# The passage between blocks of a four-layer hybrid network: token halves, prepared residual, last squares on VectorE, and stick-breaking outputs by column groups

## The chip, the cores and the metric

One core of one Trainium2 chip runs the whole network in one launch. The metric is the device time of one execution in microseconds.

## The reference

Four layers on 512 tokens of width 1024, float32. Each layer is a mixer and a convolutional FFN, both between two RMS norms:

```python
for layer in range(DEPTH):                      # 4; mixers: nsa, stick-breaking, swa, nsa
    u = rms_norm(h, norm_g[layer, 0])
    u = mixer(u, ...)                           # ends in "@ w_out", 1024 x 1024
    h = h + rms_norm(u, norm_g[layer, 1])
    u = conv_ffn(rms_norm(h, norm_g[layer, 2]), ...)   # 1024 -> 5632 -> 1024
    h = h + rms_norm(u, norm_g[layer, 3])
```

The stick-breaking mixer computes for each head, with z = q k^T / 8 and a strictly causal mask:

```python
log_1m = jnp.where(mask, jax.nn.log_sigmoid(-z), 0.0)
log_a = jax.nn.log_sigmoid(z) + lax.cumsum(log_1m, axis=3, reverse=True) - log_1m
a = jnp.where(mask, jnp.exp(log_a), 0.0)
return jnp.einsum('bhts,bshd->bthd', a.astype(v.dtype), v)
```

## The kernel before

All activations lie transposed: the model dimension on the partitions in 8 chunks of 128, the 512 tokens along the columns. `h` [128, 8, 512] is the residual, `xh` and `xl` are the high part (a reduced-precision type that TensorE takes at full rate) and the rest of the normed input. Weights come in units of 512 KB through a ring of four (`w_raw`), and ScalarE makes `w_hi` (L252, or L611 inside the FFN's loop), VectorE the rest `w_lo` (L258, L615). A product is three matmuls: w_hi xh, w_lo xh, w_hi xl (L298 to L300). A unit covers two chunks and four output banks, so 24 matmuls; a panel is four banks of PSUM, and panels alternate between banks 0 to 3 and 4 to 7. Splits of weights run three units ahead (`AHEAD`).

Each engine has its own program, written by hand; the order on an engine is the order of the code, and semaphores join them.

**The passage.** Each of the eight block outputs (mixer or FFN, numbered s = 0 to 7) is two panels of four chunks. As a bank is done, ScalarE squares it (`act_squares`, L411) and VectorE copies it to `mix_u` or `ffn_u` (`dve_take_u`, L416). GpSimd adds the squares of the first panel into `ss`. The squares of the second panel go to TensorE one by one: `pe_post` multiplies `ones` with `ss` and with each square in float32 (L395, L398), between the banks of the last unit and behind it, and so adds them over the partitions. ScalarE then forms rn = (mean + eps)^-0.5 by Ln and Exp (`act_rn`, L433 and L434). VectorE updates the residual, per chunk dh = u g rn (L454) and h += dh (L460) (`dve_update`). ScalarE writes xh = h g' (L472) and squares h (L477) (`act_update`), VectorE writes xl (L440), GpSimd adds the squares of h (`pool_h_squares`, L484 and L488). TensorE's `first_panel` starts as soon as chunk 0's xh is there: eight matmuls with xh (L319, L320), four with xl (L323), chunk by chunk. A product of `ones` with the summed squares (L370) ends the passage; the norm's factor is applied to the results behind the matmul. Seven passages join a block to the next; the eighth output is written to memory.

**Stick-breaking.** 40 tiles (head, rows of queries), two at a time. TensorE: scores of two heads in two halves of 64 rows (L1677). ScalarE: two sigmoids, `keep` (L1745) and `share` (L1748). VectorE: a backward product scan `left` (L1807) and share x left (L1813). TensorE turns the result (L1688), ScalarE copies it to `wt` (L1755), TensorE multiplies it as the stationary operand with the values `sv_t` (L1699). After ten tiles ScalarE copies the outputs to `so_t` (L1761). They have tokens on the partitions, so `pe_turn_o` turns them chunk by chunk (L1188) and ScalarE and VectorE write xh and xl (L1194, L1199) ahead of and between the units of the output panel.

## Time and profile before

| | |
|---|---|
| median of 3 runs | 2726.24 us (2725.97 to 2726.4) |
| the profiled execution | 2726.78 us, of it the span of the profile 2725.0 us |
| TensorE matmul, busy | 2620.6 us, 96% |
| VectorE, busy | 1661.9 us, 61% |
| ScalarE, busy | 1175.2 us, 43% |
| GpSimd, busy | 351.3 us, 13% |
| mean granted TensorE clock | 0.981 of 2.4 GHz |

The span goes from the first to the last instruction. Busy shares are means over stages that differ. DVE is VectorE, ACT ScalarE, POOL GpSimd, PE TensorE's matmuls, PEld its weight loads. A float32 matmul appears as two records, and TensorE's ends are modelled: a matmul's record is longer than the distance to the next.

### The profile page before, as it was taken

The page shows a single profiled execution, that of the slowest core. Times are in us where ns is not written, and L with a number is a line of the kernel's source. Part 1 is how long each engine was busy: PE and PEld are TensorE (multiplying, and loading weights), DVE is VectorE, ACT ScalarE, POOL GpSimd, SP SyncE. Part 2 cuts the span into 40 slices and gives each one's busy share as a digit, 9 for nine tenths or more (in the row PEclk, how much of TensorE's full clock was granted, in tenths as well). Part 3 has the DMA queues.
Part 4 walks back from the last instruction along what each step waited for, and adds up shares of the span by engine and source line. Part 5 has one row for each costly group of instructions (what it writes and reads, how often), then busy time and mean ns, then how long its engine had stood idle before and what let it go on. Part 6 is the DMA issues. An engine that isn't in the chain of part 4 may idle for free.

```text
span 2725.0 us, 38387 instructions
## 1 busy us (share of the span) xinstructions
PE 2620.6 (96%) x13424; PEld 2202.5 (81%) x13424; DVE 1661.9 (61%) x2844; ACT 1175.2 (43%) x1797; POOL 351.3 (13%) x298
## 2 busy tenths in 40 slices
PE   8989999999999999999999999999999899999997
PEld 6879878888778677888878878888779898788886
DVE  7567667674253857667255667773376675676733
ACT  4356544443232745444234544443333664444421
POOL 1012121110010001111010021110011121211100
PEclk9999999999999999999999999999999899999999
DMA  4400023333232012332322023323333001233331
GB/s 158 131 28 2 1 73 115 98 94 99 75 107 94 9 49 84 93 100 77 117 66 70 27 75 102 99 92 101 97 97 100 14 2 32 78 100 97 96 101 46
DMA packets 62052, 210.91 MB, mean 77 GB/s; under 512 B 8672, under 2 KB 10464, under 8 KB 61920
## 3 DMA queue, kind: packets, MB, share of 16 engines
q1 hardware_dynamic: 61920, 209.14, 24.2%
q8 instruction: 84, 1.38, 0.2%
q14 instruction: 48, 0.39, 0.0%
HBM read 207.02 MB, written 2.10 MB: 77 GB/s over the span
## 4 chain that ended last, share of the span: by engine, by line
PE 88%; DVE 7%; ACT 3%; issue 1%; DMA 0%; DVEq 0%; POOL 0%; SPq 0%; ACTq 0%; POOLq 0%
PE psum L298 20%; PE psum L300 20%; PE psum L299 20%; PE psum L970 5%; PE psum L960 3%; PE psum L814 2%; PE psum L816 2%; PE psum L815 2%; PE psum L319 2%; PE psum L950 2%; PE psum L320 2%; PE psum L949 2%; PE psum L323 2%; DVE h L460 1%; PE psum L1699 1%
## 5 line engine op out<-in xcount | busy, mean ns | idle before, releaser
L298 PE MATMUL psum<-xh,w_hi 128*128 128x512 f32 x1736 | 681.8, 393 | 5.8 <-DVEq L876 3.7
L299 PE MATMUL psum<-xh,w_lo 128*128 128x512 f32 x1736 | 677.1, 390 | 0.0
L300 PE MATMUL psum<-xl,w_hi 128*128 128x512 f32 x1736 | 677.1, 390 | 0.0
L258 DVE TENSOR_TENSOR w_lo<-w_raw,w_hi 128x1024 fp32r<-128x1024 f32 x226 | 279.8, 1252 | 511.2 <-ACT w_hi L252 509.6
L252 ACT ACTIVATE w_hi<-w_raw 128x1024 fp32r<-128x1024 f32 x226 | 235.3, 1057 | 563.2 <-PE psum L300 441.6
L298 PEld LDWEIGHTS psum<-xh,w_hi 128*128 128x128 f32 x1736 | 327.0, 188 | 76.3 <-issue 5.1
L299 PEld LDWEIGHTS psum<-xh,w_lo 128*128 128x128 f32 x1736 | 327.0, 188 | 68.9 <-issue 1.9
L300 PEld LDWEIGHTS psum<-xl,w_hi 128*128 128x128 f32 x1736 | 326.8, 188 | 68.5
L615 DVE TENSOR_TENSOR w_lo<-w_raw,w_hi 128x1024 fp32r<-128x1024 f32 x160 | 209.2, 1307 | 254.0 <-ACT w_hi L611 254.0
L298 PE MATMUL psum<-ah,w_hi 128*128 (+1 forms) x704 | 277.1, 394 | 0.0
L300 PE MATMUL psum<-al,w_hi 128*128 (+1 forms) x704 | 274.0, 389 | 0.0
L299 PE MATMUL psum<-ah,w_lo 128*128 (+1 forms) x704 | 273.9, 389 | 0.0
L611 ACT ACTIVATE w_hi<-w_raw 128x1024 fp32r<-128x1024 f32 x160 | 168.5, 1053 | 234.8 <-PE psum L300 234.8
L585 POOL TENSOR_TENSOR cv<-cv 128x512 f32<-128x512 f32 x88 | 133.8, 1521 | 786.7 <-ACT cv L539 781.3
L970 PE MATMUL psum<-v,pt 128*128 128x65 f32 x1504 | 212.5, 271 | 7.1 <-DVE pt L1066 5.5
L970 PEld LDWEIGHTS psum<-v,pt 128*128 128x128 f32 x1504 | 204.8, 194 | 16.4 <-DVE pt L1066 10.0
L534 ACT ACTIVATE cv<-xo,conv_b,conv_w 128x512 f32<-128x512 f32 x176 | 129.2, 805 | 95.5 <-DVE xo L558 95.5
L567 DVE SCALAR_TENSOR_TENSOR cv<-xo,conv_w,cv 128x512 f32<-128x512 f32 x176 | 169.5, 1003 | 0.6 <-DVE xo L558 0.6
L1110 ACT ACTIVATE scores<-scores,mins 128x256 f32<-128x256 f32 (+1 forms) x320 | 162.2, 538 | 2.5 <-DVE mins L1018 1.8
L1018 DVE CUSTOM_DVE_ANT_0 scores<-psum,tb 128x512 f32<-128x512 f32 (+3 forms) x256 | 123.4, 484 | 59.0 <-PE psum L950 58.4
L299 PEld LDWEIGHTS psum<-ah,w_lo 128*128 128x128 f32 x704 | 132.2, 188 | 29.1 <-issue 1.9
L298 PEld LDWEIGHTS psum<-ah,w_hi 128*128 128x128 f32 x704 | 132.2, 188 | 29.0 <-issue 1.9
(180 smaller groups left out, 3938.7 us busy)
## 6 DMA issues: line engine op xcount, KB each, us to landing
w_raw<-w_up SPq DMA_DIRECT2D x176, 512.0 KB, 3.6
w_raw<-w_down SPq DMA_DIRECT2D x88, 512.0 KB, 3.6
w_raw<-nsa_in SPq DMA_DIRECT2D x56, 512.0 KB, 4.2
w_raw<-sb_in SPq DMA_DIRECT2D x24, 512.0 KB, 3.6
w_raw<-nsa_out SPq DMA_DIRECT2D x16, 512.0 KB, 3.6
w_raw<-swa_in SPq DMA_DIRECT2D x10, 512.0 KB, 4.4
...
```

Of the source, the lines that this page charges most:

```text
L252: nc.scalar.activation(w_hi[:, u % RING, :], w_raw[:, u % RING, :], ACT.Copy).then_inc(hi_done, 1)
L258: nc.vector.tensor_tensor(w_lo[:, u % RING, :], w_raw[:, u % RING, :], w_hi[:, u % RING, :].bitcast(F32), ALU.subtract).then_inc(split_don ...
L298: nc.tensor.matmul(bank(p, o), wh[:, k, o, :], xhi(k), start=(first and k == 0), stop=False)
L299: nc.tensor.matmul(bank(p, o), wl[:, k, o, :], xhi(k), start=False, stop=False)
L300: mm = nc.tensor.matmul(bank(p, o), wh[:, k, o, :], xlo(k), start=False, stop=(last and k == 1))
L534: nc.scalar.activation(cv[:, o, :], xo[:, o, 2:T + 2], ACT.Identity, bias=conv_b[:, bass.ds(cc, 1)], scale=conv_w[:, 2, bass.ds(cc, 1)]).t ...
L567: marks.append(ch.then(nc.vector.scalar_tensor_tensor(cv[:, o, :], xo[:, o, 1:T + 1], conv_w[:, 1, bass.ds(cc, 1)], cv[:, o, :], ALU.mult, ...
L585: nc.gpsimd.tensor_tensor(cv[:, 2 + a, :], cv[:, a, :], cv[:, 2 + a, :], ALU.mult).then_inc(prod_done, 1)
L611: nc.scalar.activation(w_hi[:, u % RING, :], w_raw[:, u % RING, :], ACT.Copy).then_inc(hi_done, 1)
L615: nc.vector.tensor_tensor(w_lo[:, u % RING, :], w_raw[:, u % RING, :], w_hi[:, u % RING, :].bitcast(F32), ALU.subtract).then_inc(split_don ...
L970: mm = nc.tensor.matmul(psum[:, 6 + job % 2, i * (DH + 1):(i + 1) * (DH + 1)], pt[:, s % 2, j * P:(j + 1) * P], vt[b][:, k0 + j, it, :], s ...
L1110: nc.scalar.activation(sp_[:, s % 4, 0:nk * P], sp_[:, s % 4, 0:nk * P], ACT.Exp, scale=-1.0, bias=mins[:, c:c + 1]).then_inc(exp_done, 1)
```

## The change

- `pe_post` runs behind the last unit only: for each half of the tokens one float32 product of `ones` with `ss` and one with the last square. VectorE adds squares 0 to 2 of the second panel to `ss` (`dve_sum_squares`). `ones` holds 1/1024. The last bank is squared in two halves of 256 columns, and Ln and Exp run per half.
- ScalarE prepares dh[1] = g' h[0] while the output's second panel runs; VectorE adds (g g') u[0] rn to it per half (`gg` holds g g'). Chunk 0 of the next input comes from that, and TensorE starts on its first half. h[0] itself is updated behind chunk 3.
- Chunks 4 to 7 are no longer copied from PSUM (where `stays(s)` holds, that is everywhere but at the FFN output ahead of stick-breaking, s = 1, which copies them to `late_u`): the update multiplies in place in PSUM and adds from there. The panel's banks are given free at the end of the update.
- The split of the unit `AHEAD` moves: on ScalarE from before Ln to behind Exp, on VectorE from before the update to behind the update of chunk 4 and the xl of chunk 3.
- Stick-breaking: the values are now the stationary operand (64 columns), the turned shares the moving one, with two heads in the two halves of 64 columns of the array; the product over a pair waits for both copies. The outputs have the model dimension on the partitions at once, so ScalarE and VectorE write xh and xl from PSUM inside the loop, and `so_t` and its transposes go.

```diff
+                    parts = [(0, T)] if c or n == 0 else [(0, TH), (TH, T)]
+                    for lo, hi in parts:
+                        if hi < T:
+                            pe.wait_ge(xa_done, n)
+                        else:
+                            pe.wait_ge(xh_done, 8 * n + c + 1)
+                        pe.wait_ge(split_done, u + 1)
+                        for o in range(4):
+                            if o == 3 and hi < T:
+                                pe.wait_ge(r_done, 2 * n)
+                            nc.tensor.matmul(bank(p, o)[:, lo:hi], wh[:, k, o, :], xh[:, c, lo:hi], start=(c == 0 and lo == 0), stop=False,
+                                             skip_group_check=True)
+                            nc.tensor.matmul(bank(p, o)[:, lo:hi], wl[:, k, o, :], xh[:, c, lo:hi], start=False, stop=False,
+                                             skip_group_check=True)
                     pe.wait_ge(x_ready, 8 * n + c + 1)
...
-        def pe_post(pe, s, p, o):
-            if o == 2:
-                panel_free(pe, p + 1)
-                pe.wait_ge(ss_done, s + 1)
-                nc.tensor.matmul(bank(p + 1, 3), ones[:], ss[:], start=True, stop=False)
-            for c in ((), (), (0,), (1,), (2, 3))[o]:
-                pe.wait_ge(sq_done, 8 * s + 5 + c)
-                mm = nc.tensor.matmul(bank(p + 1, 3), ones[:], sq[:, c, :], start=False, stop=(c == 3))
-            if o == 4:
-                mm.then_inc(ssum_done, 1)
+        def pe_post(pe, s, p):
+            panel_free(pe, p + 1)
+            for a in range(2):
+                half = slice(TH * a, TH * a + TH)
+                pe.wait_ge(ssq_done, 3 * (s + 1))
+                nc.tensor.matmul(mean_half(p, a), ones[:], ss[:, half], start=True, stop=False)
+                if a == 0:
+                    pe.wait_ge(sqa_done, s + 1)
+                else:
+                    pe.wait_ge(sq_done, 8 * (s + 1))
+                nc.tensor.matmul(mean_half(p, a), ones[:], sq[:, 3, half], start=False, stop=True).then_inc(ssum_done, 1)
+        def mean_half(p, a):
+            return bank(p + 1, 2 + a)[:, 0:TH]
...
-                nc.scalar.activation(sq[:, o, :], bank(p, o), ACT.Square).then_inc(sq_done, 1)
+                if half and o == 3:
+                    nc.scalar.activation(sq[:, 3, 0:TH], bank(p, 3)[:, 0:TH], ACT.Square).then_inc(sqa_done, 1)
+                    nc.scalar.activation(sq[:, 3, TH:T], bank(p, 3)[:, TH:T], ACT.Square).then_inc(sq_done, 1)
+                else:
+                    nc.scalar.activation(sq[:, o, :], bank(p, o), ACT.Square).then_inc(sq_done, 1)
...
+        def stays(s):
+            return s % 2 == 0 or s + 1 == 2 * len(kinds) or kinds[(s + 1) // 2] != "sb"
...
+            def take(o):
+                if not stays(s):
+                    dve.wait_ge(sq_done, 8 * s + 5 + o)
+                    nc.vector.tensor_copy(late_u[:, o, :], bank(p, o)).then_inc(u_done, 1)
+            dve.wait_ge(ss_done, s + 1)
+            for o in range(3):
+                dve.wait_ge(sq_done, 8 * s + 5 + o)
+                dve.wait_ge(ssq_done, 3 * s + o)
+                nc.vector.tensor_tensor(ss[:], ss[:], sq[:, o, :], ALU.add).then_inc(ssq_done, 1)
+                if o < 2:
+                    take(o)
+            take(2)
+            take(3)
...
-            act.wait_ge(ssum_done, s + 1)
-            act.wait_ge(s_chain, ch.then(nc.scalar.activation(rn[:], bank(p + 1, 3), ACT.Ln, bias=eps[:], scale=1.0 / D)))
-            nc.scalar.activation(rn[:], rn[:], ACT.Exp, scale=-0.5).then_inc(r_done, 1)
-        def dve_update(dve, s, u, g_post, g_pre):
+            for a in range(2):
+                half = slice(TH * a, TH * a + TH)
+                act.wait_ge(ssum_done, 2 * s + a + 1)
+                act.wait_ge(s_chain, ch.then(nc.scalar.activation(rn[:, half], mean_half(p, a), ACT.Ln, bias=eps[:])))
+                nc.scalar.activation(rn[:, half], rn[:, half], ACT.Exp, scale=-0.5).then_inc(r_done, 1)
...
-            dve.wait_ge(r_done, s + 1)
-            for c in range(DC):
-                if c >= 2:
-                    dve.wait_ge(h_done, 8 * s + c - 1)
-                nc.vector.scalar_tensor_tensor(dh[:, c % 2, :], u[:, c, :], norm_g[:, g_post, c:c + 1],
-                                               rn[:], ALU.mult, ALU.mult).then_inc(dh_done, 1)
-                if c and g_pre is not None:
-                    dve.wait_ge(h_done, 8 * s + c)
-                    low(c - 1)
-                dve.wait_ge(dh_done, 8 * s + c + 1)
-                nc.vector.tensor_tensor(h[:, c, :], h[:, c, :], dh[:, c % 2, :], ALU.add).then_inc(h_done, 1)
-            if g_pre is not None:
+            def update(c):
+                if c < 4:
+                    src, d = u[:, c, :], dh[:, c % 2, :]
+                elif stays(s):
+                    src = d = bank(p, c - 4)
+                else:
+                    src, d = late_u[:, c - 4, :], dh[:, c % 2, :]
+                dve.wait_ge(v_chain, ch.then(nc.vector.scalar_tensor_tensor(d, src, norm_g[:, g_post, c:c + 1], rn[:], ALU.mult, ALU.mult)))
+                nc.vector.tensor_tensor(h[:, c, :], h[:, c, :], d, ALU.add).then_inc(h_done, 1)
...
-                low(DC - 1)
...
+            for a in range(2):
+                half = slice(TH * a, TH * a + TH)
+                dve.wait_ge(r_done, 2 * s + a + 1)
+                m = ch.then(nc.vector.scalar_tensor_tensor(dh[:, 0, half], u[:, 0, half], gg[:, s:s + 1], rn[:, half], ALU.mult, ALU.mult))
+                dve.wait_ge(hg_done, s + 1)
+                dve.wait_ge(v_chain, m)
+                nc.vector.tensor_tensor(dh[:, 0, half], dh[:, 0, half], dh[:, 1, half], ALU.add).then_inc(x0_done, 1)
+            dve.wait_ge(x0_done, 2 * (s + 1))
+            update(1)
+            dve.wait_ge(xh_done, 8 * (s + 1) + 1)
+            nc.vector.tensor_tensor(xl[:, 0, :], dh[:, 0, :], xh[:, 0, :].bitcast(F32), ALU.subtract).then_inc(x_ready, 1)
+            dve.wait_ge(x_ready, 8 * (s + 1) + 1)
+            update(2)
+            low(1)
+            dve.wait_ge(h_done, 8 * s + 2)
+            update(3)
+            low(2)
+            update(0)
+            for c in range(4, DC):
+                dve.wait_ge(h_done, 8 * s + c)
+                update(c)
+                low(c - 1)
+                if c == 4:
+                    split_lo(dve, u_split)
+            low(DC - 1)
+            if stays(s):
+                dve.sem_inc(evac_v, 1)
...
+                half = slice(TH * a, TH * a + TH)
+                act.wait_ge(x0_done, 2 * s + a + 1)
+                x = nc.scalar.activation(xh[:, 0, half], dh[:, 0, half], ACT.Copy)
+                if a == 0:
+                    x.then_inc(xa_done, 1)
                 else:
...
+            for k, c in enumerate((1, 2, 3, 0, 4, 5, 6, 7)):
+                act.wait_ge(h_done, 8 * s + k + 1)
+                if c:
+                    high(c)
+                square(k, c)
...
-                pe.wait_ge(wt_done, n0 + s + 1)
-                if s % 10 < 2 and s >= 10:
-                    pe.wait_ge(so_done, SB_TILES // 5 * sb_before[l] + 2 * (s // 10) + s % 2 - 1)
-                for e, i, at_ in sb_tile(s):
-                    o = 4 * DH * (e // 2 % 2) + i * DH
-                    for j in range(i + 1):
-                        mm = nc.tensor.matmul(psum[:, 6 + s % 2, o:o + DH], wt[:, s % 4, at_ + j * P:at_ + (j + 1) * P],
-                                              sv_t[:, j, e * DH:(e + 1) * DH], start=(j == 0), stop=(j == i), skip_group_check=True)
-                mm.then_inc(spv_done, 1)
+                pe.wait_ge(wt_done, n0 + s + 2)
+                if s % 10 == 0 and s >= 10:
+                    pe.wait_ge(o_ready, 8 * l + 2 * (s // 10) - 1)
+                if s % 10 == 4 and s >= 10:
+                    pe.wait_ge(o_ready, 8 * l + 2 * (s // 10))
+                both = [[(e, i, at_, j) for e, i, at_ in sb_tile(s + a) for j in range(i + 1)] for a in range(2)]
+                for q in range(len(both[0])):
+                    for a in range(2):
+                        e, i, at_, j = both[a][q]
+                        mm = nc.tensor.matmul(psum[64 * a:64 * a + 64, 6 + e // 2 % 2, i * P:(i + 1) * P], sv_t[:, j, e * DH:(e + 1) * DH],
+                                              wt[:, (s + a) % 4, at_ + j * P:at_ + (j + 1) * P], start=(j == 0), stop=(j == i),
+                                              skip_group_check=True)
+                        if q == len(both[0]) - 1:
+                            mm.then_inc(spv_done, 1)
...
-            pe_out(pe, l, so_t)
+            p, u = plan.out_p[l], plan.out_u[l]
+            x_panel(pe, p, u, l, ready=o_ready, output=True)
+            x_panel(pe, p + 1, u + 4, l, ready=o_ready, output=True)
...
+                act.wait_ge(spv_done, n0 + 10 * (c // 2 + 1))
+                nc.scalar.activation(xh[:, c, :], psum[:, 6 + c % 2, :], ACT.Copy).then_inc(oh_done, 1)
...
             for s in range(SB_TILES):
                 sticks(s)
-            dve_turn_o(dve, l, plan.out_p[l])
+                if s >= 13 and s % 10 == 3:
+                    low(s // 5 - 2)
+                    low(s // 5 - 1)
+            low(DC - 2)
+            low(DC - 1)
...
                     act_rn(act, ch, 2 * l, plan.out_p[l] + 1)
+                    split_hi(act, plan.up_u[l] + AHEAD)
                     act_update(act, 2 * l, 4 * l + 2)
```

ScalarE's order around the output of layer 0's mixer (s = 0), where the prediction's start of the passage lies. Before:

```order
L252 ACTIVATE w_hi<-w_raw 128x1024 x2
L411 ACTIVATE sq<-psum 128x512 x4
L252 ACTIVATE w_hi<-w_raw 128x1024
L433 ACTIVATE rn<-psum,eps 128x512
L434 ACTIVATE rn<-rn 128x512
L472 ACTIVATE xh<-h,norm_g 128x512
L477 ACTIVATE sq<-h 128x512
```

And the same place on ScalarE in the changed kernel (its own line numbers; L260 splits a weight):

```order
L427 ACTIVATE dh<-h,norm_g 128x512
L437 ACTIVATE sq<-psum 128x512 x3
L434 ACTIVATE sq<-psum 128x256
L435 ACTIVATE sq<-psum 128x256
L488 ACTIVATE rn<-psum,eps 128x256
L489 ACTIVATE rn<-rn 128x256
L488 ACTIVATE rn<-psum,eps 128x256
L489 ACTIVATE rn<-rn 128x256
L260 ACTIVATE w_hi<-w_raw 128x1024
L577 ACTIVATE xh<-dh 128x256 x2
```

The split has moved from ahead of Ln to between Exp and the first xh, and the last square, Ln, Exp and the first xh are in halves. VectorE in the middle of the same passage before, from the update of chunk 3 on (L454 and L460 are the update, L440 xl):

```order
L454 SCALAR_TENSOR_TENSOR dh<-mix_u,norm_g,rn 128x512
L440 SCALAR_TENSOR_TENSOR xl<-h,norm_g,xh 128x512
L460 TENSOR_TENSOR h<-h,dh 128x512
L454 SCALAR_TENSOR_TENSOR dh<-mix_u,norm_g,rn 128x512
L440 SCALAR_TENSOR_TENSOR xl<-h,norm_g,xh 128x512
```

In the changed kernel, from the update of h[0] to the xl of chunk 4 (L515 and L516 are the update, L497 xl, L266 w_lo):

```order
L515 SCALAR_TENSOR_TENSOR dh<-mix_u,norm_g,rn 128x512
L516 TENSOR_TENSOR h<-h,dh 128x512
L515 SCALAR_TENSOR_TENSOR psum<-psum,norm_g,rn 128x512
L516 TENSOR_TENSOR h<-h,psum 128x512
L497 SCALAR_TENSOR_TENSOR xl<-h,norm_g,xh 128x512
L266 TENSOR_TENSOR w_lo<-w_raw,w_hi 128x1024
L515 SCALAR_TENSOR_TENSOR psum<-psum,norm_g,rn 128x512
L516 TENSOR_TENSOR h<-h,psum 128x512
L497 SCALAR_TENSOR_TENSOR xl<-h,norm_g,xh 128x512
```

The first two of these rows are the late update of h[0]; the updates from chunk 4 on name psum where `mix_u` and `dh` stood, and w_lo is new between them. TensorE at the end of stick-breaking, before:

```order
L1688 MATMUL psum<-ident,share 128x128 x8
L1699 MATMUL psum<-sv_t,wt 128x64 x16
L1188 MATMUL psum<-ident,so_t 128x128 x16
L298 MATMUL psum<-xh,w_hi 128x512
L299 MATMUL psum<-xh,w_lo 128x512
```

In the changed kernel, at the same place:

```order
L1789 MATMUL psum<-ident,share 128x128 x8
L1803 MATMUL psum<-wt,sv_t 64x128 x16
L304 MATMUL psum<-xh,w_hi 128x512
L305 MATMUL psum<-xh,w_lo 128x512
L306 MATMUL psum<-xl,w_hi 128x512
```

The values' products now have 64 partitions by 128 columns, and the transposes of `so_t` ahead of the output panel are gone.

## Rows read from the trace of the kernel before

**Rows 1.** TensorE's waits: line, who it waited for: us, times, longest.
```profile
PE psum L319 <- ACT xh L472: 28.4, 11, 3.9
```

**Rows 2.** Timeline, first passage: start, length, engine, line, operation [idle before].
```profile
370.73 1.02 PE L395 MATMUL psum<-ss,ones 128*128 128x512 f32 x2
...
371.59 1.02 PE L398 MATMUL psum<-sq,ones 128*128 128x512 f32 x2
...
376.08 1.97 PE L398 MATMUL psum<-sq,ones 128*128 128x512 f32 x4
376.28 0.60 ACT L411 ACTIVATE sq<-psum 128x512 f32<-128x512 f32 x1 [1.64 <-PE psum L300]
376.77 1.05 ACT L252 ACTIVATE w_hi<-w_raw 128x1024 fp32r<-128x1024 f32 x1
...
378.09 0.69 ACT L433 ACTIVATE rn<-psum,eps 128x512 f32<-128x512 f32 x1 [0.27 <-PE psum L398]
...
379.47 0.75 DVE L454 SCALAR_TENSOR_TENSOR dh<-mix_u,norm_g,rn 128x512 f32<-128x512 f32 x1 [0.40 <-ACT rn L434]
...
380.98 0.72 ACT L472 ACTIVATE xh<-h,norm_g 128x512 fp32r<-128x512 f32 x1 [1.54 <-DVE h L460]
...
381.96 0.76 PE L319 MATMUL psum<-xh,w_hi 128*128 128x512 f32 x1 [3.91 <-ACT xh L472]
```

**Rows 3.** Timeline, the same passage's later part, rows of four engines.
```profile
389.12 1.78 DVE L460 TENSOR_TENSOR h<-h,dh 128x512 f32<-128x512 f32 x1
...
390.50 4.95 POOL L488 TENSOR_TENSOR ss<-ss,sq 128x512 f32<-128x512 f32 x3
...
402.66 0.72 ACT L472 ACTIVATE xh<-h,norm_g 128x512 fp32r<-128x512 f32 x1 [2.06 <-DVE h L460]
...
402.49 1.07 PE L323 MATMUL psum<-xl,w_hi 128*128 128x512 f32 x4
405.39 1.08 PE L323 MATMUL psum<-xl,w_hi 128*128 128x512 f32 x4
406.31 1.02 PE L370 MATMUL psum<-ss,ones 128*128 128x512 f32 x2
```

**Rows 4.** Groups by line and shape: a ScalarE operation of 256 columns, busy us, mean ns.
```profile
L1121 ACT ACTIVATE pt<-psum 128x256 f32<-128x256 f32 x32 | 12.1, 378 | 6.2 <-PE psum L960 5.7
```

**Rows 5.** Timeline in the first mixer: VectorE reading PSUM inside a GpSimd operation.
```profile
216.33 0.68 DVE L1018 CUSTOM_DVE_ANT_0 scores<-psum,tb 128x512 f32<-128x512 f32 x1
...
215.89 1.04 POOL L1153 TENSOR_TENSOR tb<-dist,slopes 128x512 f32<-128x512 f32 x1
```

**Rows 6.** Stick-breaking loop: timeline, one window of busy times, one line's durations.
```profile
908.42 0.60 ACT L1755 ACTIVATE wt<-psum 128x512 f32<-128x512 f32 x1 [0.83 <-PE psum L1688]
908.75 1.13 PE L1677 MATMUL psum<-sk_t,sq_t 64*128 64x512 f32 x4
...
909.87 0.62 ACT L1755 ACTIVATE wt<-psum 128x512 f32<-128x512 f32 x1
...
962.45 1.23 DVE L1807 TENSOR_TENSOR_SCAN left<-keep,own 128x512 f32<-128x512 f32 x1 [0.77 <-ACT keep L1745]
...
930.00:940.00 10.00, 9.99 (x78) 7.83 (x75) 9.48 (x16) 7.43 (x15) 0.00 (x0) 1.00 0.01 2
...
L1813 DVE TENSOR_TENSOR share<-share,left x64: 283/492/693, 891.5 to 974.2; 128x512 f32<-128x512 f32 x16, 128x384 f32<-128x384 f32 x16, 128x128 f32<-128x128 f32 x16, 128x256 f32<-128x256 f32 x16
```

**Rows 7.** Timeline, end of stick-breaking and the output's first unit.
```profile
975.15 3.68 PE L1699 MATMUL psum<-sv_t,wt 128*128 128x64 f32 x32
...
975.35 0.60 ACT L1755 ACTIVATE wt<-psum 128x512 f32<-128x512 f32 x1 [1.33 <-PE psum L1688]
...
982.95 0.47 PE L298 MATMUL psum<-xh,w_hi 128*128 128x512 f32 x1 [1.47 <-DVE xl L1199]
...
988.52 1.04 PE L1188 MATMUL psum<-ident,so_t 128*128 128x128 f32 x8
```

**Rows 8.** Window: length, busy of PE, PEld, DVE, ACT, POOL, clock, DMA share, GB/s.
```profile
898.00:900.00 2.00, 1.12 (x6) 0.80 (x6) 1.90 (x3) 1.56 (x4) 0.00 (x0) 0.50 0.00 0
```

142 lines of the change are left out of this document (79 added, 63 removed).

## The prediction

> **What bounds the kernel now.** I read the page first, then the list of waits, then the timeline of single stretches. TensorE is the long engine, so only what it loses counts. The list of waits says where it loses most: 28.4 us at the first product of a passage, in 11 waits, the longest 3.9 [rows 1]. There are seven passages (four mixer outputs and the first three FFN outputs hand a new residual to the next first panel), and 7 x 3.9 = 27.4, so the four other waits are together 1 us. The eighth FFN output goes to the result.
>
> The timeline of the first passage shows the chain [rows 2]. Two float32 sum products begin at 370.73 and the next at 371.59, so one of 512 columns costs 0.86 us (two records). Three of them (ss, then squares 0 and 1) stand between the banks of the last unit; two follow the last product. I call 376.08, when the last two begin, P: the products are over there. The square of bank 3 starts at P + 0.20 and lasts 0.60, Ln starts at P + 2.01, VectorE at P + 3.39, the first xh at P + 4.90, the first product at P + 5.88. That product's record is 0.76 long; after the shorter gap at 982.95 it is 0.47 [rows 7], so the clock had fallen here and not there.
>
> Later in the passage [rows 3] TensorE needs 2.9 us from one group of four xl products to the next (402.49 to 405.39; 2.72 where it waits for nothing, as 12 products of 0.227), and the passage ends with the product over ss at 406.31 = P + 30.23. Meanwhile VectorE is slowed: with GpSimd adding squares (three adds in 4.95 us) an add to h takes 1.78 us, where the longest product of this width in the stick-breaking loop, with GpSimd idle, takes 693 ns [rows 6]. The last xh is written at 402.66, which is when TensorE gets to that chunk. So VectorE's chain and TensorE's work end together: time saved at the front is kept only as far as VectorE keeps up. That decides this change.
>
> In the stick-breaking loop [rows 6] VectorE is busy 9.48 us of 10, with 20 pairs of tiles from 891.5 to 974.2, some 4.1 us a pair.
>
> **Part by part, sums between banks.** The three products of 0.86 leave the last unit; VectorE adds squares 0 to 2 instead (0.69 each, in the place of three copies of the same length, while a bank takes 6 x 0.227 = 1.36). Gain 2.6 us in each of eight outputs.
>
> **Front of the passage.** Half width costs ScalarE 378 ns where full width costs 0.60 [rows 4], so a half saves 0.22; I take the same off 0.69, 0.72 and 0.75. The half square ends at P + 0.58. From the square's end (376.88) to Ln 1.21 us pass now, 0.86 of them the product; with half a product 0.78, so Ln is at P + 1.36. From Ln to VectorE it is 1.38 now, less two times 0.22: P + 2.3, and the second half has r at about P + 3.2. VectorE has x0's first half at P + 3.27. But ScalarE now has the weight copy (1.05 us, at 376.77 in rows 2) between Exp and xh; it ends at P + 4.25. So xh half 0 ends at P + 4.78 and the first product is at P + 5.0, 0.9 before. That copy was free behind the last sum product; here it costs about 1 us of the start, and I expect that to be hidden again by the next wait. The 16 half products replace 8 full ones, at 0.12 to 0.2 each: nil to 1 us.
>
> **Back of the passage.** VectorE: four half operations to P + 4.2, chunks 1, 2, 3 (1.4 each with 0.7 for each xl), the update of chunk 0 to P + 11.7, chunk 4 to P + 13.1. GpSimd starts on its first four squares after chunk 0's, P + 12.4, and has four or five adds in a row to do. From there the xl's and the weight difference w_lo, which is now here instead of ahead of the passage (1.23 us), each take turns with GpSimd at 1.7. Updates 4 to 7 read and write PSUM. The nearest rows are a VectorE operation from PSUM of 0.68 us inside a GpSimd operation of 1.04 [rows 5]: not stretched. So I take 1.4 us for them. The row has PSUM as a source only; if they are stretched too, each costs up to 1.1 more. The Trainium skill, "SBUF — State Buffer", section "SBUF: two separate sides", has VectorE and GpSimd lock a shared pair of ports when VectorE has two SBUF inputs; by that rule too these updates go free, and the trace agrees (0.68 against 1.78).
> With this: xl3 is written at P + 14.4, w_lo at P + 16.7, h5 at P + 18.1, xl4 at P + 19.9, h6 P + 21.4, h7 P + 23.5, xl7 P + 25.4. TensorE at full clock would be ready for xl4 at P + 17.8 (5.0 + 1.9 + 0.9 + 3 x 2.72 + 1.8), waits until 20.0, then runs 0.9 + 3 x 2.72: end at P + 29.1. Should the clock fall in the gap of 3 us as it does now, the first chunk costs 2 us more and the wait swallows them. So the end moves from 30.23 to 29.1: gain 1.1.
> The passage into stick-breaking keeps a copy in SBUF (`late_u`), its updates are stretched as now, and with h7 near P + 27.6 it ends at about P + 31.3: a loss of 1.0.
> Sum: six passages x (2.6 + 1.1) = 22.2, one x (2.6 - 1.0) = 1.6, tail 2.6 + 0.1 = 2.7.
>
> **Stick-breaking.** In the loop VectorE gets six xl subtractions of 0.69, in three places: +1.3 us each. Now it waits 0.77 for `keep` there [rows 6], because ScalarE drains the outputs first; the subtractions fill that wait, but the outputs also come later, since the products over a pair now wait for both copies. I take +0.8 each, +2.4; bounds 0 and +4. The pair product V is now 3.68 / 2 = 1.84 us [rows 7]. Two heads side by side: the nearest row is the scores, 2 x 2 records of 512 columns in 64-row halves, 1.13 us [rows 6] where one after the other is 4 x 0.43 = 1.7. So V is between 0.85 and 1.9; I take 1.1. It matters by another route: the first copy waits for the transposes, the second starts 1.45 later (908.42 and 909.87 [rows 6]) and lasts 0.6, then V, then half of the transposes and 0.2: a round of 2.75 + V. With 1.1 that is 3.85, under VectorE's 4.1. With 1.9 it is 4.65, and 20 rounds lose 11 us.
> End: the last copy ends at 975.95 [rows 7], V later (977.05) the products of x start, instead of at 982.95: 5.9; the two later groups of 8 transposes (1.04 the record, some 0.9 without its tail) go: 1.8. Net -5.9 - 1.8 + 2.4 = -5.3, rounded to -5.
>
> **Total.** 22.2 + 1.6 + 2.7 + 5 = 31.5. The profiled execution took 2726.78 (span 2725.0), the median of the runs is 2726.24, 0.5 lower. 2726.2 - 31.5 = **2695**.
>
> **Rivals.**
> A, TensorE keeps its lead: GpSimd's turns hit VectorE less than I say (w_lo or xl4 a slot earlier), and the passage ends when TensorE has no wait, P + 26.9. Against: all seven passages show the stretched adds. Six more times 2.2 = 13 less: 2682.
> B, updates on PSUM are stretched as well: like the passage into stick-breaking, all seven end at P + 31.3. 6 x 2.1 = 13 more: 2708. For: no row writes PSUM from VectorE. Against: rows 5.
> C, the heads are not side by side, V = 1.9: 11 us more in the loop and 0.8 at its end, 2707. For: each product has its own weights to load. Against: the scores' row. On it the Trainium skill speaks against this change: "TensorE: Matmul & The Clock Gate", Part 3, says that a weight load overlaps a running matmul only where the row groups differ, and these pairs share all rows; by that C is the outcome, and no row here shows column halves.
> D, slower than before: TensorE, with a third of each round idle, drops to the half clock in the loop and stays. At 898 to 900 it ran at 0.50 with 1.12 us busy of 2 [rows 8]. Then transposes (0.9), scores (1.0) and products (1.1) take 2 x 3.0 = 6.0 against 4.1 a round, 1.9 lost, 38 in 20 rounds: 2695 + 38 = 2733. It outweighs the 31.5 us of the rest from 17 rounds on, with the serial V of C (2 x 3.8 = 7.6, 3.5 lost) from 9 on. Against: from 902 on the clock is full although TensorE waits at each output.
> E, the change of front brings nothing at all, since the end of VectorE's chain stays: only the 2.6 x 8, 5 in stick-breaking: 2700. It lies in my range.
>
> **How the numbers follow.** Forecast with E: 0.52 (own range 2689 to 2701). A 0.15, B 0.13, C 0.15, D 0.05. Range 2683 to 2710 takes in most of A, and B and C; outside lie D, the far end of A, and B with C together: under 2 in 10. 0.2% (5.4 us) is what a measurement tells from no change. All cases but D give 16 us or more; B with C and an undersized saving between banks could come near it: faster 0.92, same 0.04, slower 0.04.
>
> **What would show it.** Right: no sum products between banks, first product near P + 5.0, w_lo and xl4 at 1.7 us each, a wait of about 2 us on xl4 (a new row: TensorE at the xl products behind VectorE), end near P + 29; updates 4 to 7 at 0.7 to 0.8; pair products 1.1 us. Wrong: PSUM updates at 1.7 (B), V at 1.8 and `wt` waits in every round (C), clock under 1 from 905 on (D), or TensorE without waits after chunk 0 (A).

## The result and the profile after

| | before | after |
|---|---|---|
| median (lowest to highest), 4 runs each | 2726.32 (2725.97 to 2727.27) us | 2695.19 (2692.94 to 2697.17) us |
| profiled execution, span | 2726.78, 2725.0 us | 2692.94, 2691.2 us |

The ratio is 0.9889, 95% interval 0.9877 to 0.9901. The medians differ by 31.1 us; 2695 was predicted. The parts fit less well than the sum, as the passages show. One run of the experiments, of the kernel with both copies ahead, took 4312 us at a mean granted clock of 0.56; its ratio leaves it out, and nothing here explains it.

TensorE's waits after the change (line, who it waited for: us, times, longest):

```profile
PE psum L332 <- ACT xh L577: 17.4, 7, 2.6
PE psum L1789 <- DVE share L1916: 16.2, 22, 1.4
PE psum L338 <- DVE xl L497: 10.0, 8, 2.3
```

and one row of before:

```profile
PE psum L1688 <- DVE share L1813: 4.4, 6, 1.3
```

The first row answers to [rows 1]: 28.4 us have become 17.4. One row is new: the products over `xl` wait for VectorE's low parts (10.0 us). Another has grown: stick-breaking's transposes waited 4.4 us for `share` and now wait 16.2, since TensorE has less to do in a round.

The first passage, front (start, length, engine, line, operation [idle before]):

```profile
371.27 0.39 PE L306 MATMUL psum<-xl,w_hi 128*128 128x512 f32 x1
371.69 0.38 ACT L434 ACTIVATE sq<-psum 128x256 f32<-128x256 f32 x1 [0.76 <-PE psum L306]
...
372.94 0.47 ACT L488 ACTIVATE rn<-psum,eps 128x256 f32<-128x256 f32 x1 [0.59 <-PE psum L416]
...
373.89 0.48 DVE L531 SCALAR_TENSOR_TENSOR dh<-mix_u,gg,rn 128x256 f32<-128x256 f32 x1 [2.24 <-ACT rn L489]
...
374.63 1.04 ACT L260 ACTIVATE w_hi<-w_raw 128x1024 fp32r<-128x1024 f32 x1
...
375.58 0.71 ACT L577 ACTIVATE xh<-dh 128x256 fp32r<-128x256 f32 x2
...
376.23 0.36 PE L332 MATMUL psum<-xh,w_hi 128*128 128x256 f32 x1 [2.47 <-ACT xh L577]
```

P, the end of the last unit's products, is the last product's start and 0.23: 371.50. Against [rows 2] Ln is at P + 1.44 (before 2.01), VectorE at 2.39 (3.39), the first product at 4.73 (5.88), and chunk 0's xh waits for the weight copy (L260) as foreseen.

The same passage, later part:

```profile
384.37 1.30 POOL L591 TENSOR_TENSOR ss<-sq 128x512 f32<-128x512 f32 x1 [22.59 <-ACT sq L564]
384.39 0.69 DVE L516 TENSOR_TENSOR h<-h,psum 128x512 f32<-128x512 f32 x1
...
385.81 5.23 POOL L595 TENSOR_TENSOR ss<-ss,sq 128x512 f32<-128x512 f32 x3
386.14 2.31 DVE L266 TENSOR_TENSOR w_lo<-w_raw,w_hi 128x1024 fp32r<-128x1024 f32 x1
...
388.37 0.75 DVE L515 SCALAR_TENSOR_TENSOR psum<-psum,norm_g,rn 128x512 f32<-128x512 f32 x1
389.15 0.69 DVE L516 TENSOR_TENSOR h<-h,psum 128x512 f32<-128x512 f32 x1
389.76 1.83 DVE L497 SCALAR_TENSOR_TENSOR xl<-h,norm_g,xh 128x512 fp32r<-128x512 f32 x1
...
391.65 1.20 PE L338 MATMUL psum<-xl,w_hi 128*128 128x512 f32 x4 [0.82 <-DVE xl L497]
...
400.87 1.02 PE L386 MATMUL psum<-ss,ones 128*128 128x512 f32 x2
```

Beside GpSimd's adds the updates on PSUM keep their length (0.75, 0.69), while `w_lo` takes 2.31 and the xl of chunk 4, called xl4 here, 1.83. TensorE waits for xl4, and the passage ends at P + 29.37; in [rows 3] it was P + 30.23.

Not every passage went so. This is the third, out of stick-breaking, P = 1015.86:

```profile
1035.99 1.74 PE L338 MATMUL psum<-xl,w_hi 128*128 128x512 f32 x4 [2.33 <-DVE xl L497]
...
1037.53 0.63 PE L332 MATMUL psum<-xh,w_hi 128*128 128x512 f32 x1
```

and its windows (length, busy PE, PEld, DVE, ACT, POOL, clock, DMA share, GB/s):

```profile
1030.00:1036.00 6.00, 3.67 (x18) 2.65 (x16) 5.96 (x6) 1.98 (x4) 5.38 (x5) 1.00 0.29 84
1036.00:1041.00 5.00, 5.00 (x15) 3.96 (x16) 4.93 (x7) 2.82 (x5) 2.61 (x3) 0.66 0.01 4
```

Chunk 0 of the first and of the third passage:

```profile
376.20:379.20 3.00, 2.97 (x18) 2.90 (x19) 2.90 (x5) 1.33 (x3) 0.00 (x0) 0.74 0.02 5
1020.60:1023.60 3.00, 3.00 (x21) 2.83 (x22) 2.90 (x5) 1.30 (x3) 0.00 (x0) 1.00 0.00 0
```

In the third passage chunk 0 ran at full clock (in the first it was 0.74 over 3 us), TensorE came to xl4 sooner, waited 2.33 us for the same slot of VectorE, and then the clock fell to the 1.2 GHz level (a record 0.63 long in place of 0.39). The xl4 products start at P + 20.1 in both passages, but this one ends at P + 30.95. The table has, from each run's timeline, first product and end (start of the product over `ss`, L386) behind P:

| passage | before | after |
|---|---|---|
| 1, 4, 5, 6, 7 | 5.88 to 5.89, end 30.22 to 30.28 | 4.73 to 4.90, end 29.34 to 29.38 |
| 3 | 5.88, end 30.24 | 4.74, end 30.95 |
| 2, into stick-breaking | 5.88, end 30.49 | 5.12, end 32.09 |

Stick-breaking, timeline of a round of the loop and of its end:

```profile
922.30 0.62 ACT L1861 ACTIVATE wt<-psum 128x512 f32<-128x512 f32 x1
...
923.22 1.09 PE L1803 MATMUL psum<-wt,sv_t 128*64 128x128 f32 x16
...
926.39 0.62 ACT L1861 ACTIVATE wt<-psum 128x512 f32<-128x512 f32 x1
...
969.14 3.13 PE L1803 MATMUL psum<-wt,sv_t 128*64 128x128 f32 x32
969.24 0.60 ACT L1861 ACTIVATE wt<-psum 128x512 f32<-128x512 f32 x1 [1.90 <-PE psum L1789]
972.20 0.50 PE L304 MATMUL psum<-xh,w_hi 128*128 128x512 f32 x1
```

One line's durations (ns min/median/max, first and last start):

```profile
L1916 DVE TENSOR_TENSOR share<-share,left x64: 284/492/694, 885.0 to 967.6; 128x512 f32<-128x512 f32 x16, 128x384 f32<-128x384 f32 x16, 128x128 f32<-128x128 f32 x16, 128x256 f32<-128x256 f32 x16
```

A window at the end:

```profile
968.00:972.00 4.00, 3.90 (x36) 3.57 (x36) 0.05 (x1) 0.60 (x1) 0.00 (x0) 0.57 0.00 0
```

A pair's 16 products take 1.09 us, the round is 4.1 as before, and from first to last `share` the loop takes 82.6 us where [rows 6] has 82.7. At its end the mean granted clock is 0.57 for 4 us, so the x products start 2.36 after the last copy's end (969.84), not 1.1.

**Where the 33.8 us between the two profiled spans went.** Counted from one P to the next, less the passages themselves: the sums between banks 2.6 to 2.7 in each output (2.73 in the last: from the seventh P to the end of the span 388.03 us less the passage's 30.22, and after 384.42 less 29.34), 21.2 in all; five passages 0.88 each, the third -0.7, the second -1.6, together 2.1; stick-breaking 6.1. That leaves 4.4, which no edit explains: the mixers of the first and last layer are shorter by about 2 and 2.6. Up to the first P the trace of before has 17.1 us at half clock and that of after 13.7; between the sixth passage's end and the seventh P it is 20.5 and 17.1 (for one, the product at 70.08 is 0.63 long before, 0.39 after). The other kernels with the sums moved have their first P between 371.84 and 374.01, so the 371.50 of this trace is at the favourable edge.

### The profile page after: what moved, and what is told of

Same layout as the page of the kernel before. It is cut to its first block, busy times and chain, and to the rows that moved or that the text cites. A ratio compares the mean times of both kernels' runs of the same rounds, so it can differ in the third digit from the quotient of the medians.

```text
span 2691.2 us, 38440 instructions
## 1 busy us (share of the span) xinstructions
PE 2576.8 (96%) x13432; PEld 2176.4 (81%) x13432; DVE 1652.7 (61%) x2869; ACT 1178.2 (44%) x1827; POOL 354.6 (13%) x298
## 4 chain that ended last, share of the span: by engine, by line
PE 84%; DVE 12%; ACT 2%; issue 1%; DMA 0%; DVEq 0%; POOL 0%; SPq 0%; ACTq 0%; POOLq 0%
PE psum L304 20%; PE psum L305 20%; PE psum L306 20%; PE psum L1073 6%; PE psum L1063 3%; PE psum L917 2%; PE psum L918 2%; PE psum L919 2%; DVE left L1910 2%; PE psum L1053 2%; PE psum L1052 2%; PE psum L338 1%; DVE h L516 1%; DVE w_lo L266 1%; DVE xl L497 1%
## 5 line engine op out<-in xcount | busy, mean ns | idle before, releaser
L266 DVE TENSOR_TENSOR w_lo<-w_raw,w_hi 128x1024 fp32r<-128x1024 f32 x226 | 288.7, 1291 | 520.5 <-ACT w_hi L260 518.8
L260 ACT ACTIVATE w_hi<-w_raw 128x1024 fp32r<-128x1024 f32 x226 | 235.5, 1057 | 572.9 <-PE psum L306 450.6
L720 DVE TENSOR_TENSOR w_lo<-w_raw,w_hi 128x1024 fp32r<-128x1024 f32 x160 | 209.2, 1308 | 253.6 <-ACT w_hi L716 253.6
L306 PEld LDWEIGHTS psum<-al,w_hi 128*128 128x128 f32 x704 | 132.2, 188 | 27.5
```

The costliest lines, as they stand in the source:

```text
L260: nc.scalar.activation(w_hi[:, u % RING, :], w_raw[:, u % RING, :], ACT.Copy).then_inc(hi_done, 1)
L266: nc.vector.tensor_tensor(w_lo[:, u % RING, :], w_raw[:, u % RING, :], w_hi[:, u % RING, :].bitcast(F32), ALU.subtract).then_inc(split_don ...
L306: mm = nc.tensor.matmul(bank(p, o), wh[:, k, o, :], xlo(k), start=False, stop=(last and k == 1))
L720: nc.vector.tensor_tensor(w_lo[:, u % RING, :], w_raw[:, u % RING, :], w_hi[:, u % RING, :].bitcast(F32), ALU.subtract).then_inc(split_don ...
```

## Experiments

Each kernel is the changed one with one edit unless said otherwise. Ratios are to the kernel before on the same chip, 4 or 5 runs to 9. "Ends" are of passages 1, 3, 4, 5, 6, 7 behind P, in that order; passage 2 stands apart.

**Stick-breaking's share**: the products with the values, the copy to `so_t` and its transposes as before.

```diff
-                nc.scalar.activation(xh[:, c, :], psum[:, 6 + c % 2, :], ACT.Copy).then_inc(oh_done, 1)
...
+                nc.scalar.activation(pair[:, :, c % 2, :, :], psum[:, 6 + c % 2, :].rearrange("p (e t d) -> p e t d", e=2, d=DH),
+                                     ACT.Copy).then_inc(so_done, 1)
...
-            x_panel(pe, p, u, l, ready=o_ready, output=True)
+            pe_out(pe, l, so_t)
```

> The changed kernel with the stick-breaking output of before (values head after head into rows of tokens, copied, transposed again at the end), all else as changed. The trace of after, laid over that of before, gives stick-breaking 6.1 us (7.1 between the second and the third passage's P, less 2.6 - 1.6 for the sums and the second passage). If that is stick-breaking's own, this kernel takes 2695.2 + 6.1 = 2701.3, and the mean round of its loop is 4.1 us, as with the column groups. If instead the subtractions in the loop cost what the prediction put on them (2.4), undoing them wins that back and it takes 2699. If the gain came from the clock of the stretch alone, it takes 2696 to 2697.

2705.22 us, ratio 0.9926 (0.9912 to 0.9939): 4 more than the 2701.3 expected. From the second passage's end to the third's P it took 249.6 us, where after took 244.7: 4.9 us for the edit. The rest is passages: ends 29.3, 30.9, 30.8, 29.4, 30.9, 29.4, and 33.0 into stick-breaking. So three of six fell into the later ending although nothing there was touched, and the ending is not a property of the third passage.

**The sums alone**, on the kernel before: VectorE adds squares 0 to 2, the two products stand behind the last unit.

```diff
+                if half and o < 3:
+                    dve.wait_ge(ss_done, s + 1)
+                    dve.wait_ge(ssq_done, 3 * s + o)
+                    nc.vector.tensor_tensor(ss[:], ss[:], sq[:, o, :], ALU.add).then_inc(ssq_done, 1)
                 nc.vector.tensor_copy(u[:, 4 * half + o, :], bank(p, o)).then_inc(u_done, 1)
```

> The kernel before with one thing changed: VectorE adds squares 0 to 2 of an output to ss, and TensorE has only the two products after the last unit. Theory of the prediction: 2.6 us in each of 8 outputs, 20.8 in all, 2726.3 - 20.8 = 2705.5, and every passage from P to its end as before, 30.2 us. Rival: VectorE, now with an add and a copy of 0.69 each for a bank of 1.36, comes to the last copies late, ss is ready late, and 0.7 us of each output go to a wait of the products behind it: 2711.

2703.81 us, ratio 0.9921 (0.9907 to 0.9934), 21.5 us less. This edit alone is two thirds of the whole change. The first product is 0.3 later (P + 6.17), the ends 30.5 to 30.6: in the first passage VectorE, with adds and copies, ends its third add at P + 0.16, and the product over `ss` starts at P + 0.31 and not at P.

**Both copies ahead.** The weight copy on ScalarE before Ln and `w_lo` before x0, as before the change.

```diff
             act_squares(act, 2 * l, 1, plan.out_p[l] + 1, u + 8)
+            split_hi(act, u + 8 + AHEAD)
...
             dve_sum_squares(dve, 2 * l, plan.out_p[l] + 1)
+            split_lo(dve, u + 8 + AHEAD)
...
-                if c == 4:
-                    split_lo(dve, u_split)
```

> The changed kernel with the weight copy and its difference w_lo back where they stood before the change: the copy on ScalarE between the last square and Ln, w_lo on VectorE ahead of x0. In the trace of after w_lo takes 2.3 us in front of h5 and xl4, and TensorE waits 0.6 to 2.3 us on xl4 in all seven passages. Theory: w_lo is that wait. Without it xl4 is there 1.7 to 2.3 us sooner, Ln is 0.4 later and the first product no later than now, and the passages end at about P + 27.9 in place of 29.4: 7 x 1.5 = 10 less, 2685. Rival: the slots of VectorE and GpSimd move together, the adds that w_lo met meet xl4 and xl5 instead, and a passage wins 0.5 at most: 2692. Third: Ln waits a whole copy (1.04) and chunk 0 starts that much later, nothing is won: 2695.

2685.20 us, ratio 0.9854 (0.9836 to 0.9872). The median is of four runs with the one of 4312 us among them; of the other three it is 2683.20. Ends 28.3, 28.1, 28.2, 28.2, 28.1, 28.1, and 31.1. In the sixth passage (P = 1930.96) both sit nearly in idle time: Ln starts 0.24 later behind P than in the changed kernel and VectorE 0.58 later, but no copy stands ahead of the first xh, and the first product is at P + 4.68. The back runs without `w_lo`:

```profile
1931.70 1.06 ACT L260 ACTIVATE w_hi<-w_raw 128x1024 fp32r<-128x1024 f32 x1
...
1932.64 0.47 ACT L488 ACTIVATE rn<-psum,eps 128x256 f32<-128x256 f32 x1
1932.79 1.23 DVE L266 TENSOR_TENSOR w_lo<-w_raw,w_hi 128x1024 fp32r<-128x1024 f32 x1 [1.67 <-ACT w_hi L260]
...
1947.56 1.83 DVE L497 SCALAR_TENSOR_TENSOR xl<-h,norm_g,xh 128x512 fp32r<-128x512 f32 x1
```

**Which of the two copies?** Only the one on ScalarE ahead:

> The changed kernel with only ScalarE's weight copy back ahead of Ln; w_lo stays behind xl3, where the change put it. Tells which of the two copies the gain of the copies ahead belongs to. Theory: the wait on xl4 is w_lo's, so the ends stay at P + 29.4 or 30.9 as in after, though the first product comes 0.3 sooner (P + 4.45): 2694 to 2696. Rival: it was the weight copy between Exp and xh that held the whole chain, and without it the ends come to P + 28.2: 2685 to 2687.

2699.12 us, ratio 0.9894 (0.9878 to 0.9911). First product at P + 4.36 to 4.52, ends 31.0, 29.6, 29.6, 31.1, 29.6, 31.0, and 33.0, xl4 at 20.4 in the six. TensorE starts 0.37 earlier, but VectorE starts 0.26 later (P + 2.65, Ln stands behind the copy), and xl4 and the ends follow VectorE: 0.2 later. So the weight copy alone brings nothing; the gain of the copies ahead needs `w_lo` ahead.

**`w_lo` later**, behind xl5 (`if c == 6` for `if c == 4`):

> The changed kernel with one line moved: w_lo behind xl5 (two updates later), the weight copy where the change put it. The unit is first needed at chunk 6. Theory that w_lo's place is the wait: xl4 comes 1.7 to 2.3 us sooner, the wait on it goes, w_lo is done by P + 23 when TensorE gets to chunk 6, and the passages end at about P + 27.9: 2685, as with the copies ahead. Rival: VectorE has no slack before chunk 6 either and the same wait reappears at chunk 6 or xl6: 2693 to 2695.

2690.24 us, ratio 0.9871 (0.9856 to 0.9886): between the two theories. Ends 29.1 in all six, 32.1 into stick-breaking. The wait on xl4 is gone, but `w_lo` met GpSimd again. The first passage (P = 372.57):

```profile
393.19 1.52 POOL L595 TENSOR_TENSOR ss<-ss,sq 128x512 f32<-128x512 f32 x1 [0.17 <-ACT sq L564]
393.49 2.30 DVE L266 TENSOR_TENSOR w_lo<-w_raw,w_hi 128x1024 fp32r<-128x1024 f32 x1
...
395.94 0.47 PE L332 MATMUL psum<-xh,w_hi 128*128 128x512 f32 x1 [1.12 <-DVE w_lo L266]
```

It is ready 1.12 us after chunk 6 wants it. With this wait in the place of the one on xl4 all six ended alike.

**GpSimd's adds thinned.** The first add stays whole, the later ones cover 8 of 512 columns, so this kernel leaves out most of the sum of squares that the norm needs.

```diff
-                nc.gpsimd.tensor_tensor(ss[:], ss[:], sq[:, c % 4, :], ALU.add).then_inc(ssh_done, 1)
+                nc.gpsimd.tensor_tensor(ss[:, 0:8], ss[:, 0:8], sq[:, c % 4, 0:8], ALU.add).then_inc(ssh_done, 1)
```

> The changed kernel with GpSimd's six later adds of the squares of h cut to 8 of 512 columns in every passage (the sums are then not those of the reference), the first add whole; all waits stay. Theory: VectorE's slots of 1.7 to 2.3 us behind chunk 4 are GpSimd's adds and nothing else. Without them VectorE's chain has xl4 at P + 17.8 in place of 20.1 to 22.1, TensorE waits for nothing behind chunk 0, and a passage ends at P + 28.2 where the clock falls in chunk 0 and at P + 26.7 where it doesn't, the passage into stick-breaking too (now 32.1): 6 x 1.2 to 2.7 and 4 to 5.4, so 11 to 21 less, 2674 to 2684. Rival: VectorE's slots are its own (w_lo, PSUM sources), the wait on xl4 stays near 2 us: 2693 to 2695.

2679.14 us, ratio 0.9829 (0.9816 to 0.9843). Ends 27.2 five times, 28.2 once (clock fallen in chunk 0), 28.6 into stick-breaking.

```profile
387.28 1.22 DVE L266 TENSOR_TENSOR w_lo<-w_raw,w_hi 128x1024 fp32r<-128x1024 f32 x1
...
389.81 0.74 DVE L497 SCALAR_TENSOR_TENSOR xl<-h,norm_g,xh 128x512 fp32r<-128x512 f32 x1
...
390.61 1.19 PE L338 MATMUL psum<-xl,w_hi 128*128 128x512 f32 x4 [0.16 <-DVE xl L497]
```

`w_lo` is 1.22 and xl4 0.74 long in the very place that the changed kernel has them. The slots are GpSimd's adds. In the passage into stick-breaking the one long operation left is an add of `h` and `dh` beside the first, whole add: 1.82 us, the later ones 0.69.

**PSUM or SBUF.** Two more passages (the fourth and the sixth) update chunks 4 to 7 from copies in SBUF:

```diff
-            return s % 2 == 0 or s + 1 == 2 * len(kinds) or kinds[(s + 1) // 2] != "sb"
+            return s % 2 == 0 or s + 1 == 2 * len(kinds)
```

> The changed kernel with chunks 4 to 7 copied to SBUF and updated from there in two more passages (the ones into the third and fourth mixer), as in the passage into stick-breaking. In after that passage ends at P + 32.1 and the others at 29.4 (one at 30.9). Theory: updates on PSUM go beside GpSimd's adds at full speed (0.75 and 0.69 us), those from SBUF take turns (1.77 and 1.82), and that is the 2.7: both passages end at P + 32.1, 5.4 slower, 2700.5. Rival: the passage into stick-breaking is late for another reason (the panel behind it, its weights), and the two stay at 29.4: 2695.

2698.41 us, ratio 0.9908 (0.9894 to 0.9923). Those two end at 31.7 (32.1 expected), the others at 29.4 or 30.9 (two each), the one into stick-breaking at 32.1. The fourth (P = 1385.51):

```profile
1398.41 1.82 DVE L516 TENSOR_TENSOR h<-h,dh 128x512 f32<-128x512 f32 x1
...
1401.85 2.31 DVE L266 TENSOR_TENSOR w_lo<-w_raw,w_hi 128x1024 fp32r<-128x1024 f32 x1
...
1404.08 1.77 DVE L515 SCALAR_TENSOR_TENSOR dh<-late_u,norm_g,rn 128x512 f32<-128x512 f32 x1
...
1407.28 1.20 PE L338 MATMUL psum<-xl,w_hi 128*128 128x512 f32 x4 [2.30 <-DVE xl L497]
```

The same two operations that took 0.75 and 0.69 on PSUM take turns with GpSimd here. xl4 is multiplied at P + 21.8 in place of 20.1. Chunk 0 kept full clock in both, and the clock did not fall behind the wait of 2.3 us.

**The clock at the front**: eleven small products in TensorE's idle time.

```diff
+            if s < 2 * len(kinds) - 1:
+                for q in range(11):
+                    nc.tensor.matmul(bank(p + 1, 0)[:, 0:P], ones[:], ones[:], start=True, stop=True)
```

> The changed kernel with eleven products of 128 columns more (ones by ones, 0.2 us each, into a bank that nothing reads) behind the sum products of seven outputs, so that TensorE works through most of the 3 us ahead of the first product. In the passages of after the granted clock falls in one of two places: in chunk 0, then the passage ends at P + 29.4 (five of six), or, where chunk 0 kept full clock, behind the wait of 2.3 us on xl4, then it ends at P + 30.9 (one of six; 32.1 in the passage into stick-breaking). Theory: a fall in chunk 0 is swallowed by the wait on xl4, one behind that wait is not. With chunk 0 at full clock in all passages TensorE only comes sooner to a wait that VectorE ends, and falls there: all at P + 30.9, 5 x 1.5 = 8 us slower than after, 2703. Rival: TensorE without its idle time at the front keeps full clock to the end, and the passages end at P + 29.4 as now or sooner: 2690 to 2695.

2695.71 us, ratio 0.9891 (0.9875 to 0.9906). Chunk 0 had full clock in every passage, and TensorE waited 2.3 us on xl4 in every one. Ends 29.3, 30.9, 29.3, 29.4, 30.9, 30.8, and 33.0 into stick-breaking. So half of my theory fell: after the wait the clock falls in some passages and stays in others (windows 1.00 from 393, 0.72 from 1035.5):

```profile
1035.50:1041.50 6.00, 5.29 (x16) 4.20 (x17) 5.83 (x8) 3.33 (x6) 3.43 (x4) 0.72 0.10 40
393.00:399.00 6.00, 6.00 (x28) 4.96 (x27) 5.47 (x8) 4.17 (x6) 3.64 (x3) 1.00 0.00 0
```

The rival fell too: a faster chunk 0 brought nothing. Where no fall came at all the passage ends at 29.3, as it does with a fall in chunk 0.

Without the filling the two places go together more closely than that. In the four kernels that leave this stretch as the change has it (after, stick-breaking as before, heads in turn below, and the four passages without copies above) there are 22 passages beside the ones into stick-breaking. In 12 the clock fell in chunk 0, the wait on xl4 was 0.6 to 1.0 us and the end 29.4. In the other 10 chunk 0 kept full clock, the wait was 2.3 us, the clock fell behind it and the end was 30.8 to 30.9. With the weight copy ahead three of four such waits were followed by a fall, with the filled front three of six.

The same filling **with both copies ahead**:

> The kernel with both copies ahead, and the eleven products of 128 columns in TensorE's idle time ahead of the first product. With the copies ahead alone the passages ended at P + 28.1 where chunk 0 ran at full clock and at 28.2 to 28.3 where the clock fell in it. Theory: VectorE's chain sets the end there too, so the clock of chunk 0 is worth 0.1 to 0.2 a passage: within 1 us of the copies ahead alone, 2684 to 2685. Rival: full clock from the first product on lets TensorE run ahead, a passage wins the 1.5 of a fallen chunk: 2675.

2682.45 us, ratio 0.9844 (0.9830 to 0.9857); six ends at 28.1. It can't be told from the copies ahead alone, as expected. These two kernels beat both the kernel before and the changed one.

**Without token halves**, in the changed kernel and with the copies ahead:

> The changed kernel without the token halves: one square of bank 3, one pair of sum products of 512 columns, one Ln, Exp, x0 and xh for chunk 0. All else as changed. By the durations of full width in the trace of before, VectorE has x0 at P + 4.8 in place of 4.2 and the first product is at P + 5.6 in place of 4.7. Theory: VectorE's chain sets the end, so the 0.6 pass to it: passages end at P + 30.0, seven times 0.6 is 4.3, 2699.5. Rival: TensorE waits on xl4 for GpSimd's turns and not for the start of the chain, and the halves bring nothing: 2695.

> The kernel with both copies ahead, without the token halves. In the changed kernel undoing the halves moved the first product from P + 4.74 to 6.24 and the end from 29.4 (or 30.9) to 30.3 to 30.75. Theory: half of the 1.5 was the copy in the place between Exp and xh; with the copies ahead the first product is at P + 5.6 against 4.7, VectorE's chain is 0.7 later, and so are the ends, 28.9: seven times 0.7, 5 more than with the halves, 2690. Rival: as without halves in the changed kernel, 1.5 at the start and 1 at the end: 2692. Third: TensorE's lead hides it: 2685.

In the changed kernel 2696.93 us, ratio 0.9903 (0.9888 to 0.9918): no difference to after that can be told. Ends 30.3, 30.3, 30.3, 30.8, 30.6, 30.3, and 33.6. With the copies ahead 2695.26 us, ratio 0.9889 (0.9874 to 0.9904): by the ratios 10 us slower than with halves, twice what I expected. Ends 29.7, 29.7, 30.5, 30.6, 30.5, 29.6, and 31.4. In both the first product is at P + 6.24, 1.5 later: with copies ahead, Ln, Exp, the two operations of x0 and xh follow each other at full width.

```profile
374.60 0.69 ACT L475 ACTIVATE rn<-psum,eps 128x512 f32<-128x512 f32 x1 [0.56 <-PE psum L409]
375.38 0.63 ACT L476 ACTIVATE rn<-rn 128x512 f32<-128x512 f32 x1
...
376.04 0.75 DVE L516 SCALAR_TENSOR_TENSOR dh<-mix_u,gg,rn 128x512 f32<-128x512 f32 x1 [0.75 <-ACT rn L476]
376.93 0.69 DVE L519 TENSOR_TENSOR dh<-dh 128x512 f32<-128x512 f32 x1
377.65 0.63 ACT L558 ACTIVATE xh<-dh 128x512 fp32r<-128x512 f32 x1 [1.65 <-DVE dh L519]
```

P is 372.30 here. My 0.9 had counted the half off some of the five steps and not off all. The clock has a part in the 10 us too. With the copies ahead and the halves it stayed full through three of these six passages. Without the halves it fell in all six, for about 3 us in three of them and for over 6 us in the three that end at 30.5 and 30.6, and TensorE no longer waited on xl4. How much of the 10 us is the clock and how much the longer steps is not separated here.

**Heads one after the other** (`for a in range(2)` outside `for q in range(len(both[0]))`):

> The changed kernel with the products of a stick-breaking pair in another order: the eight of one head's tile, then the eight of the other's, in place of alternating between the two column halves. In after 16 products take 1.09 us. Theory: that is because two that stand side by side run together; one half after the other costs 1.9 to 2.2, the round goes from 4.1 to 4.65 or more, 20 rounds lose 11 us: 2706. Rival: each product costs the same alone (0.06), and the order is nothing: 2695. Third: the products grow to 1.9, but VectorE still sets the round, and only the last pair's products show: 2696.

2699.21 us (2690.61 to 2700.09), ratio 0.9895 (0.9881 to 0.9910). A pair grew from 1.09 to 1.58:

```profile
927.63 1.58 PE L1803 MATMUL psum<-wt,sv_t 128*64 128x128 f32 x16
...
929.14 0.66 PE L1789 MATMUL psum<-ident,share 128*128 128x128 f32 x4
```

but the stretch from the second passage's end to the third's P took 243.7 us (after 244.7), so the loop lost nothing. The single records show what runs side by side. In after the products of the two heads start 0.006 us apart and the next two 0.102 later; in turn, the products of one head start 0.109 apart, and the second head's first product starts while the first head's are still going. So the heads do run side by side, and this kernel doesn't need it. The ends are 30.9, 29.4, 30.9, 30.9, 29.4, 30.9, and 33.0.

## Why the prediction was right, and where its parts were not

**Sums between banks** (2.6 x 8): right. 21.2 in the traces. The run with this alone is 21.5 faster; in its trace the passages gave 1.8 back, and its last mixer is 3.5 shorter than before's for no reason in the edit, as that of after is 2.6 shorter.

**Front of the passage**: right in order and nearly in size. First product at P + 4.73 (5.0), Ln at 1.44 (1.36), VectorE at 2.39 (2.3), chunk 0's xh held by the copy. "Expected to be hidden by the next wait" fits the run with the weight copy ahead: 0.37 earlier at the start, nothing won at the end.

**Back of the passage**: the mechanism was right. xl4 was written at P + 20.1 (19.9 forecast), TensorE waited for it in all seven, and the end of five was 29.4 (29.1). `w_lo` takes 2.31, not the 1.7 that the text names, but the sum had 2.3 for it (xl3 at 14.4, `w_lo` at 16.7), so this moved nothing. What was mis-sized is the clock. I let a fall in the first gap be swallowed by the wait, which holds (ends 29.4), but did not ask what the clock does behind that wait where chunk 0 has kept it. Of the 22 passages counted above 12 ended near 29.4 and 10 near 30.9, a mean of 30.1. Before, 30.25. The gain of 1.1 a passage that the sum took six times is on average nearer 0.2: rival E, that the front brings nothing, was closer to this part than the forecast.

**Passage into stick-breaking**: a loss of 1.0 forecast, 1.6 found, 2.5 where the clock fell. VectorE's copies between the adds make its front later as well (the product over `ss` starts at P + 0.68, the first product at 5.12).

**Stick-breaking** (-5): 4.9 by the run without it, 6.1 by the traces. Right for partly wrong reasons. V was 1.1 (1.09). The 2.4 for subtractions in the loop did not come: VectorE waited 5.4 us for `keep` in six places before, 2.1 in two after, and the six subtractions went into that. In its place the end gained less than 5.9: from the last `share` to the first x product 4.2 less (before 974.60 to 982.95, after 968.05 to 972.20), the clock having fallen there. The two later groups of transposes gave the 1.8 as forecast.

**Rivals.** A and B are refuted (waits on xl4 in every passage; 0.75 and 0.69 beside GpSimd). C is refuted: V was 1.09. Even with V at 1.58 the round held 4.1, so 2.75 + V was 0.2 too long; V = 1.9 was never reached. By the Trainium skill, "TensorE: Matmul & The Clock Gate", Part 3, weight loads overlap a running product only where row groups differ. The trace does not agree: these halves share all rows, and the 16 loads of a pair, from 923.22 on, cover 0.85 of the 1.09 us of its products. Alternating the heads took 1.09 us where one after the other took 1.58. D happened in small: 0.57 over 4 us at the loop's end, some 1.2 us (2.36 in place of 1.1). By the Trainium skill, "SBUF — State Buffer", "SBUF: two separate sides", a VectorE operation with two SBUF inputs and a GpSimd operation that reads SBUF lock a shared pair of ports against each other. The rows above agree: PSUM updates are free (0.75 and 0.69), those from `late_u` (1.77), `w_lo` (2.31) and xl4 (1.83) are stretched, and `w_lo` and xl4 are short again with the adds thinned (1.22 and 0.74).

**The total**: 31.5 forecast, 31.1 measured. In the two traces the passages brought 2.1 where 5.6 was forecast. Stick-breaking brought 1.1 more than forecast, and the 4.4 us at the clock of the first and last mixer, which no term of the sum foresaw, more than filled the rest. That the total fits to 0.4 us is in this part luck. Kernels that differ from after only where it should cost nothing (filled front, ScalarE's copy ahead, heads in turn) have ratios of 0.9891 to 0.9895, so a typical value lies nearer 2697.

Open is what decides in which passages chunk 0 keeps its clock, with the same work and the same gap ahead of it, and why the clock stays full behind some waits of 2.3 us. With the filled front it fell behind three of six.
